# Twelve modulation blocks of the second layer moved out of the heads, border sums on VectorE, and a last residual by tokens

## The chip, the cores and the metric

One core of one Trainium2 chip runs one launch of the kernel. The metric is the time of the device in microseconds (us), the median over runs; less is better. Three runs of the kernel before gave a median of 1421.49 us (1420.72 to 1425.16).

## The reference

A block of two layers works on 256 tokens of x and 256 of a context, width 1024, all in float32. Cut to what matters:

```python
for l in range(DEPTH):                      # 0: HGRN mixer, 1: mamba mixer
    last = l == DEPTH - 1
    mx = split((silu(c) @ ada_w[l] + ada_b[l]), 6)          # modulation of x
    mc = split(silu(c_ctx) @ ada_w[l] + ada_b[l], 6)        # and of the context
    hx, hc = modulate(rmsnorm(x, pre[l,0]), mx[0], mx[1]), modulate(rmsnorm(ctx, pre[l,0]), mc[0], mc[1])
    yx, yc = mixer[l](hx, hc)
    x = x + mx[2] * rmsnorm(yx, post[l,0]);   ctx likewise with mc[2], if not last
    hx = modulate(rmsnorm(x, pre[l,1]), mx[3], mx[4])
    yx = (silu(conv(hx @ w_up[:, :2816])) * (hx @ w_up[:, 2816:])) @ w_down
    x = x + mx[5] * rmsnorm(yx, post[l,1]);   ctx likewise, if not last
return x                                     # 256 x 1024
```

ada_w is 2 x 1024 x 6144: 48 MB in all, or 24 blocks of 1024 x 512 (2 MB), twelve to a layer. Of each layer, columns 0 to 1023 are the shift before the mixer, then scale, gate, and the same three for the FFN.

## The kernel before, in words

**Layout.** Activations are held transposed: xT and yT are [128, 8, 512], 8 feature tiles of 128 by 512 tokens (256 of the context, 256 of x). From the mamba output on only the 256 tokens of x are left. Weights stream from HBM in pieces of 512 KB (two rows of tiles, `wraw`); ScalarE (ACT) rounds each to `wh` (`split_hi`, line 779), VectorE (DVE, line 1288) or GpSimd (POOL, line 654) takes the rest `wl`, and TensorE (PE) makes each product of float32 from three matmuls, hh·wh, hl·wh, hh·wl (lines 2052 to 2054, or 2067 to 2069 where the inputs arrive one by one).

**Order.** Everything is written out by hand. Each engine runs its own program, and a planner (`plan.add(key, bank, reader)`) only gives PSUM banks and the counts of the semaphores. Loads stand in one list on the queue of SP, each with a wait for its buffer; an engine's instructions run strictly in the order written.

**Stages.** (1) start, (2) eight heads of the HGRN mixer, some 42 us each, (3) its output product y0 to y7, then **border A**, the end of the mixer and the begin of FFN 0, (4) FFN 0, whose last tile opens **border B**, (5) mamba groups g = 0 to 7 with two steps more that drain the pipeline, (6) its output product (`("y", 1, m)`), **border C**, (7) FFN 1 with `up` and `down` in two halves, (8) the end: residual, transposition to rows of tokens, store.

**Modulation.** Block n goes through four steps. `load_ada(n)` on SP brings two halves of 1 MB into `araw`. `ada_block(n)` on PE multiplies the silu of the two conditions with it (line 2118, 8 instructions in the order of the program, 16 in the trace). `ada_rows(n)` copies the sums out (ACT, line 852). `ada_turn(n)` is four transposes on PE (line 2130), and `ada_add(n)` two small ones on DVE (lines 1298 and 1303) that finish `mod`. `norm_scales` and `gate_scales` then form nsc and gsc. How many blocks a head takes is in `ada_of`; those behind the heads are numbered from LATE on. `araw` and `scc` lie on the stack of the HGRN stage, so no block can stand behind it.

**Borders.** rmsnorm of the mixer's output, residual and the next rmsnorm are folded: three sums over features are needed, of y² (`ss`), of B = y·gsc·x (`sb`) and of A = (gsc·y)² (`sa`). For each tile m, ACT squares y (line 786) and gsc·y (`scaled_square`, line 823), DVE forms and adds up B (lines 1355 and 1360), POOL adds up the two squares (lines 709 and 718). PE sums over partitions with `ones` (lines 2340 and 2342). `variance` (lines 1369 to 1380) and `add_and_norm` (1393 to 1408) follow, and their first results release FFN's first matmul (line 2067).

**End.** `residual` forms y·rstd on 256 columns (line 1333, and 726 on POOL) and xT + gsc·that (line 1343) tile by tile; PE transposes 16 blocks (line 2588), ACT and DVE copy four banks, and SP stores two pieces of 512 KB.

Of the kernel before, what the change touches and what calls it, by code (L numbers as in the profile page):

```python
# [18 lines left out]
P = 128  # L19
# [113 lines left out]
def program(nc, a, out):  # L133
# [22 lines left out]
    gsc = sb(ctx, "gsc", [P, 2, 2, KT, 2])  # L156
    ident = sb(ctx, "ident", [P, P])
# [8 lines left out]
    mbs = sb(ctx, "mbs", [64, 3])  # L166
    asum = sb(ctx, "asum", [P, 2, 512])
# [16 lines left out]
    araw = sb(hg, "araw", [P, 2, 4, 512])  # L184
    scc = sb(hg, "scc", [P, KT, 32])
# [74 lines left out]
    ada_of = [1, 2, 2, 2, 2, 2, 2, 2]  # L260
# [86 lines left out]
    def plan_ffn(l):  # L347

        for half in range(2):
            ffp[l, half, "up"] = plan.loop(2 * FH[half], {"dve": 2 * FH[half]})  # L350
            if half == 0:
                if l == 0:
                    plan.add(("at", LATE + 3), 6, "dve")
                    plan.add(("at", LATE + 4), 7, "dve")
                ffp[l, half, "down"] = plan.loop(KT, {"act": KT})
            else:
                for m in range(KT):
                    plan.add(("fy", l, m), 4 + m % 2, "dve")

    plan_ffn(0)  # L360
    plan_sums(0, 1, (0, 1))
    ring = {"g": 0, "s": 0}
# [6 lines left out]
    for g in range(GROUPS + 2):  # L369
# [11 lines left out]
        if g == 1:  # L381
            mkey(("tk", 0), "dve")
# [7 lines left out]
        if G:  # L390
            gkey(("b", g), "dve")
        if S:
# [4 lines left out]
        if g == 0:  # L397
            plan.add(("c", g), 7, "dve")
        elif G:
            gkey(("c", g), "dve")  # L400
        if Q:
            mkey(("yt", q), "act")
        if S:
            mkey(("off", p, 0), "dve")
            mkey(("off", p, 1), "dve")
        if G:
# [3 lines left out]
    for m in range(KT):  # L410
        plan.add(("y", 1, m), m % 3, "act")
    plan_sums(1, 0, (4, 5))
    plan_ffn(1)
    plan.add(("ss", 1, 1), 7, "act")
    for half in range(2):
        for t in range(2):
            plan.add(("out", t, half), 2 * t + half, ("act", "dve")[half])
# [73 lines left out]
    scales, rsq_ready = sem("scales"), sem("rsq_ready")  # L491
    a_ready, a_added, b_added, var_ready = sem("a_ready"), sem("a_added"), sem("b_added"), sem("var_ready")
    x_new = sem("x_new")
    hf_ready, hh_ready, hl_ready = sem("hf_ready"), sem("hh_ready"), sem("hl_ready")
    yl_ready, odd_ready = sem("yl_ready"), sem("odd_ready")
# [21 lines left out]
    rows_act, rows_dve = sem("rows_act"), sem("rows_dve")  # L517
# [27 lines left out]
    def ada_half(n, half):  # L545
# [6 lines left out]
        return afirst[half], a_landed[half], 16 * (n - 1)  # L552
# [9 lines left out]
    def _(sp):  # L562
# [14 lines left out]
        def load_ada(n):  # L577

            l, c = ada_order[n] // 12, 512 * (ada_order[n] % 12)
            user = n - 2 if n <= ADA_FIRST else n - 1  # L580
            for half in range(2):
                if n == LATE + 4:
                    plan.wait_ready(sp, ("ot", HEADS - 1))
                elif user >= 0:
# [31 lines left out]
        load_ada(LATE + 4)  # L616
        for n in range(5 * HEADS + SLOTS + 4, len(subs)):
            load(n)
        for t in range(2):
            sp.wait_ge(rows_act, t + 1)  # L620
            sp.wait_ge(rows_dve, t + 1)
            sp.dma_start(out[0, t * P:(t + 1) * P, :], rows_out[:, t, :]).then_inc(stored, 16)
        sp.wait_ge(stored, 32)
# [3 lines left out]
    def _(pool):  # L627
# [29 lines left out]
        def split_rest(l, w):  # L657

            for half in range(2):
# [31 lines left out]
                else:  # L691
                    for m in range(KT):
                        add_square(2 * l + 1, m, w)
                        if l == 0:
                            add_scaled(1, m, w)
# [15 lines left out]
        def add_scaled(n, m, w):  # L711

            A = a_sums[n]
            if 1 <= m < KT - 1:
                pool.wait_ge(a_ready, KT * n + m + 1)
                if m > 1:
                    pool.wait_ge(a_added, (KT - 2) * n + m - 1)
                pool.tensor_tensor(A[m % 2][:, 0:w], A[m % 2][:, 0:w], A[1 - m % 2][:, 0:w], ALU.add).then_inc(a_added, 1)

        def scale_odd(n, w):  # L720

            pool.wait_ge(rstd_ready, 2 * n + 2)
            for m in range(1, KT, 2):
                if m >= 2:
                    pool.wait_ge(x_new, KT * n + m - 1)
# [1890 lines left out]
```

## Time and profile before

| | |
|---|---|
| runs (3) | median 1421.49 us, 1420.72 to 1425.16 |
| profiled execution | 1424.4 us, its span 1422.7 us |
| PE busy | 1332.8 us, 94% |
| DVE busy | 903.5 us, 64% |
| ACT busy | 660.9 us, 46% |
| POOL busy | 355.2 us, 25% |
| DMA | 183.15 MB, mean 129 GB/s |
| chain that ended last | PE 77%, DVE 11%, ACT 6%, DMA 3%, issue 2% |

All numbers of single instructions come from the profiled execution. Its time lies 2.9 us above the median, and 1.7 us of it lie outside the span. A row of the timeline reads: start in us from the span's start, duration in us, engine, line, operation, tiles out<-in, partitions x elements, count, and in brackets how long the engine sat idle before it and who released it. Matmuls overlap, so what one costs is the distance of starts, not its duration.

### The profile page before, as it was taken

To read this page: it belongs to the slowest core of one execution; us is meant where nothing else is said; L and a number is where in the kernel's file an instruction comes from. 1 tells how busy PE (TensorE), PEld (TensorE's weight loads), DVE (VectorE), ACT (ScalarE), POOL (GpSimd) and SP (SyncE) were. 2 spreads that over 40 slices of the span, in tenths; PEclk is the share of its full clock that TensorE was granted. 3 is DMA by queue.
4 is the path that set the end of the run, shared out by engine and by line. 5 is a ranking of instruction groups with operands and counts; after the bars stand their busy time and mean duration, and the time that the engine had idled before them with its cause. 6 is when DMAs were issued, how large, how long until landed. Compare 5 with 4: busy or idle time off the path is not lost.

```text
span 1422.7 us, 21240 instructions
## 1 busy us (share of the span) xinstructions
PE 1332.8 (94%) x7879; PEld 1119.1 (79%) x7879; DVE 903.5 (64%) x1678; ACT 660.9 (46%) x1050; POOL 355.2 (25%) x243
## 2 busy tenths in 40 slices
PE   5999999999987999999999978999999978899996
PEld 2677877777764788888888847888888877899996
DVE  5667765667759744422445788677777856764564
ACT  4444444444455633223333456555555645654552
POOL 1000000000231455104551500211111321681952
PEclk9999999999999999999999988999999989999998
DMA  9565445457542233234322324233333235456642
GB/s 346 168 193 178 160 137 178 130 182 236 179 161 76 74 106 94 74 96 118 97 83 63 104 59 114 80 89 90 101 92 90 74 90 149 119 162 186 198 137 86
DMA packets 274483, 183.15 MB, mean 129 GB/s; under 512 B 6595, under 2 KB 249059, under 8 KB 274403
## 3 DMA queue, kind: packets, MB, share of 16 engines
q1 hardware_dynamic: 273858, 180.00, 42.1%
q10 hardware_dynamic: 544, 2.10, 0.4%
q8 instruction: 49, 0.80, 0.2%
q14 instruction: 32, 0.25, 0.1%
HBM read 181.03 MB, written 1.05 MB: 128 GB/s over the span
## 4 chain that ended last, share of the span: by engine, by line
PE 77%; DVE 11%; ACT 6%; DMA 3%; issue 2%; SPq 1%; POOL 1%; POOLq 0%; DVEq 0%; ACTq 0%
PE bank L2052 20%; PE bank L2054 20%; PE bank L2053 20%; DVE wl L1288 2%; PE bank L2118 2%; ACT tmp L834 1%; DMA gates<-in_ada_w 1%; DMA araw<-in_ada_w 1%; ACT wh L779 1%; DVE hl L1388 1%; DVE tmp L1408 1%; PE bank L2167 1%; DVE conv L1739 1%; PE bank L2567 1%; PE bank L2542 1%
## 5 line engine op out<-in xcount | busy, mean ns | idle before, releaser
L2052 PE MATMUL bank<-hh,wh 128*128 128x512 f32 (+1 forms) x1305 | 464.9, 356 | 16.0 <-DVE wl L1288 10.8
L2054 PE MATMUL bank<-hh,wl 128*128 128x512 f32 (+1 forms) x1305 | 459.8, 352 | 0.0
L2053 PE MATMUL bank<-hl,wh 128*128 128x512 f32 (+1 forms) x1305 | 459.4, 352 | 0.0
L779 ACT ACTIVATE wh<-wraw 128x1024 fp32r<-128x1024 f32 (+2 forms) x265 | 256.3, 985 | 97.3 <-PE bank L2054 92.2
L2052 PEld LDWEIGHTS bank<-hh,wh 128*128 128x128 f32 x1305 | 249.6, 191 | 51.5 <-DVE wl L1288 13.6
L1288 DVE TENSOR_TENSOR wl<-wraw,wh 128x1024 fp32r<-128x1024 f32 (+2 forms) x187 | 209.8, 1144 | 124.6 <-ACT wh L779 124.6
L2054 PEld LDWEIGHTS bank<-hh,wl 128*128 128x128 f32 x1305 | 249.4, 191 | 33.1
L2053 PEld LDWEIGHTS bank<-hl,wh 128*128 128x128 f32 x1305 | 249.6, 191 | 30.8
L1739 DVE SCALAR_TENSOR_TENSOR conv<-bank,pv,conv 128x189 f32<-128x189 f32 (+3 forms) x396 | 173.2, 437 | 132.5 <-ACT conv L1056 104.3
L654 POOL TENSOR_TENSOR wl<-wraw,wh 128x1024 fp32r<-128x1024 f32 x78 | 187.1, 2408 | 236.4 <-ACT wh L779 235.8
L2052 PE MATMUL bank<-fh,wh 128*128 128x512 f32 (+1 forms) x352 | 119.7, 340 | 3.9 <-DVE wl L1288 3.5
L2054 PE MATMUL bank<-fh,wl 128*128 128x512 f32 (+1 forms) x352 | 119.0, 338 | 0.0
L2053 PE MATMUL bank<-fl,wh 128*128 128x512 f32 (+1 forms) x352 | 119.0, 338 | 0.0
L701 POOL TENSOR_TENSOR hl<-yT,hh 128x512 fp32r<-128x512 f32 x13 | 19.2, 1503 | 385.9 <-DVE gates L1635 374.8
L753 POOL TENSOR_TENSOR wx<-xtok,wtk 128x512 f32<-128x512 f32 x16 | 16.9, 1057 | 248.1 <-ACT xtok L1179 159.8
L2052 PEld LDWEIGHTS bank<-fh,wh 128*128 128x128 f32 x352 | 66.2, 188 | 12.5 <-issue 2.1
L2054 PEld LDWEIGHTS bank<-fh,wl 128*128 128x128 f32 x352 | 66.2, 188 | 8.0
L2053 PEld LDWEIGHTS bank<-fl,wh 128*128 128x128 f32 x352 | 66.2, 188 | 7.9
L2067 PE MATMUL bank<-hh,wh 128*128 128x512 f32 (+2 forms) x119 | 47.6, 400 | 21.1 <-DVE hl L1388 18.8
L674 POOL TENSOR_TENSOR fl<-prod,fh 128x512 f32 (+3 forms) x44 | 50.0, 1135 | 55.1 <-ACT fh L1072 55.1
L1056 ACT ACTIVATE conv<-bank,pv 128x512 f32<-128x512 f32 (+1 forms) x44 | 29.4, 668 | 71.7 <-PE bank L2054 71.7
L709 POOL TENSOR_TENSOR sq<-sq 128x512 f32<-128x512 f32 (+1 forms) x24 | 27.3, 1138 | 107.9 <-ACT sq L786 107.9
(325 smaller groups left out, 1960.5 us busy)
## 6 DMA issues: line engine op xcount, KB each, us to landing
wraw<-in_ffn_w_up SPq DMA_DIRECT2D x88, 512.0 KB, 3.9
araw<-in_ada_w SPq DMA_DIRECT2D x42, 1024.0 KB, 7.2
wraw<-in_mb_w_in SPq DMA_DIRECT2D x48, 512.0 KB, 4.0
wraw<-in_hg_w_in SPq DMA_DIRECT2D x40, 512.0 KB, 4.2
wraw<-in_ffn_w_down SPq DMA_DIRECT2D x32, 512.0 KB, 3.8
wraw<-in_mb_w_out SPq DMA_DIRECT2D x16, 512.0 KB, 4.2
gates<-in_ada_w SPq DMA_DIRECT2D x5, 1024.0 KB, 10.7
wraw<-in_hg_w_out SPq DMA_DIRECT2D x8, 512.0 KB, 5.9
```

The costliest lines, as they stand in the source:

```text
L654: pool.tensor_tensor(wl[:, n % SLOTS, 0:size], wraw[:, n % SLOTS, 0:size], wh[:, n % SLOTS, 0:size].bitcast(F32), ALU.subtract).then_inc(w ...
L674: pool.tensor_tensor(fl[:, bass.ds(i * 2 + c, 1), 0:w], prod[:, c % 2, 0:w].unsqueeze(1), fh[:, bass.ds(i * 2 + c, 1), 0:w].bitcast(F32), ...
L709: pool.tensor_tensor(sq[:, m % 2, 0:w], sq[:, m % 2, 0:w], sq[:, 1 - m % 2, 0:w], ALU.add).then_inc(sq_added, 1)
L779: act.activation(wh[:, n % SLOTS, 0:size], wraw[:, n % SLOTS, 0:size], ACT.Copy).then_inc(w_hi, 1)
L1056: act.activation(conv[:, u, 0:n], bank[2 * u if src is None else src][:, 0:n], ACT.Identity, scale=pv[:, bass.ds(i * 2 + (cw + c), 1)], bi ...
L1288: ins = dve.tensor_tensor(wl[:, s, lo:hi], wraw[:, s, lo:hi], wh[:, s, lo:hi].bitcast(F32), ALU.subtract)
L1739: ins = V.scalar_tensor_tensor(out=o(conv[:, u, :]), in0=src(bank[up]), scalar=pv[:, bass.ds(i * 2 + (cw + row * FT + c), 1)], in1=o(conv[ ...
L2052: pe.matmul(dst, W, hi(k), start=(k == 0), stop=False, **skip)
L2053: pe.matmul(dst, W, lo(k), start=False, stop=False, **skip)
L2054: ins = pe.matmul(dst, L, hi(k), start=False, stop=(k == nk - 1), **skip)
L2067: pe.matmul(dst, W, hi(k), start=(k == 0), stop=False, skip_group_check=True)
L2118: ins = pe.matmul(bank[plan.bank(key)][32 * j:32 * j + 32, :], scc[:, 4 * half + j, :], raw[:, j, :], start=(half == 0), stop=(half == 1))
```

## The change

1. `ada_of` is [1, 1, 1, 1, 1, 1, 1, 1], so LATE falls from 19 to 12. The blocks LATE to LATE+4 stay at the places of the program where five stood before. Seven more get places: LATE+5 and +6 behind the sums of border B (turns in g = 0, before and behind project("c")), LATE+7 in g = 1, LATE+8 in g = 8, LATE+9 in g = 9 (turn behind y tile 1), LATE+10 behind y tile 1 (turn behind tile 3), LATE+11 ahead of FFN 1 (turn after its first `up` half). Their loads are put into SP's list behind given weight loads (`after`). `araw` and `scc` lie below all stages now. LATE+6 lands in `rows_out`, `prod` and `tmp`.
2. At the three borders DVE forms A itself, from ACT's y² and gsq = gsc², and adds up y²: lines 1370 and 1381 of the changed kernel. `scaled_square`, `add_scaled` and POOL's `add_square` there go, and so does one of PE's two sum matmuls for A. At border A the splits of y tiles 5 to 7 stand one tile earlier, as far as they did not already.
3. At the end ACT scales y by gsc into `conv`, PE transposes that (two 128x128 a tile, `y_rows`) and xT (`x_rows`, four for each of tiles 0 to 3) inside the `down` loop, ACT copies the latter to rows_out. The sum of squares comes out per token (four matmuls of one column, `token_sums`), ACT's Ln and Exp work on 128x2, four DVE instructions of 128x512 form bank·rstd + rows_out, and four stores of 256 KB follow.

The diff, cut to its core:

```diff
-    ada_of = [1, 2, 2, 2, 2, 2, 2, 2]
+    ada_of = [1, 1, 1, 1, 1, 1, 1, 1]
...
+        after = {at["up", 0, 0, 0, 0] + 12: (LATE + 5,), at["down", 0, 1, 0, 0] + 7: (LATE + 6,), at["z", 0, 0]: (LATE + 7,),
+                 at["z", 2, 0]: (LATE + 8,), at["m", 3, 1]: (LATE + 9, LATE + 10), at["m", 4, 1]: (LATE + 11,)}
         for n in range(5 * HEADS + SLOTS + 4, len(subs)):
             load(n)
+            for late in after.get(n, ()):
+                load_ada(late)
...
-                        if l == 0:
-                            scaled_square(1, 0, 1, m, n)
+                        if l == 1:
+                            if m >= 2:
+                                act.wait_ge(gy_used, m - 1)
+                            act.activation(conv[:, m % 2, 0:n], yT[:, m, 0:n], ACT.Copy, scale=gsc[:, 1, 1, m, 0:1])\
+                                .then_inc(gy_ready, 1)
+                            if m < 4:
+                                t, h = m // 2, m % 2
+                                key = ("xr", t, h)
+                                plan.wait_ready(act, key)
+                                plan.empty(act.activation(rows_out[:, t, h * 512:h * 512 + 512], bank[6][:, :], ACT.Copy), "act", key)
...
-                step(ins)
-                step.wait()
-                ins = V.tensor_tensor(B[m % 2][:, 0:n], B[m % 2][:, 0:n], B[1 - m % 2][:, 0:n], ALU.add)
-            ins.then_inc(b_added, 1)
+                product = step(ins)
+            else:
+                ins.then_inc(b_added, 1)
+            A, S = a_sums[i], sq[:, m % 2, :]
+            dve.wait_ge(sq_ready, KT * i + m + 1)
+            if m:
+                dve.wait_ge(a_added, KT * i + m)
+            for b in range(n // SEQ):
+                r = slice(b * SEQ, (b + 1) * SEQ)
+                g2 = gsq[:, l, s, m, b:b + 1]
+                if m:
+                    ins = V.scalar_tensor_tensor(out=A[m % 2][:, r], in0=S[:, r], scalar=g2, in1=A[1 - m % 2][:, r],
+                                                 op0=ALU.mult, op1=ALU.add)
+                else:
+                    ins = V.tensor_scalar(A[0][:, r], S[:, r], g2, None, ALU.mult)
+            ins.then_inc(a_added, 1)
+            if 1 <= m < KT - 1:
+                step.wait(product)
+                V.tensor_tensor(B[m % 2][:, 0:n], B[m % 2][:, 0:n], B[1 - m % 2][:, 0:n], ALU.add).then_inc(b_added, 1)
+                dve.wait_ge(a_added, KT * i + m + 1)
+                if m > 1:
+                    dve.wait_ge(sq_added, (KT - 2) * i + m - 1)
+                V.tensor_tensor(S[:, 0:n], S[:, 0:n], sq[:, 1 - m % 2, 0:n], ALU.add).then_inc(sq_added, 1)
...
+                if (l, s, m) == (0, 1, 0):
+                    plan.wait_ready(dve, ("am", LATE + 6))
...
-        residual(1, 1, SEQ)
+        dve.wait_ge(rstd_ready, rn[0] + 1)
+        plan.wait_emptied(dve, ("xr", 1, 1))
+        for half in range(2):
+            for t in range(2):
+                key = ("out", t, half)
+                plan.wait_ready(dve, key)
+                o = rows_out[:, t, half * 512:half * 512 + 512]
+                plan.empty(V.scalar_tensor_tensor(out=o, in0=bank[plan.bank(key)][:, :], scalar=rstd[:, t:t + 1], in1=o,
+                                                  op0=ALU.mult, op1=ALU.add), "dve", key)
...
@@ down loop of ffn_pe @@
+                            ada_block(LATE + 5)
+                            ada_block(LATE + 6)
...
+                        if l == 1:
+                            if m < 4:
+                                x_rows(m // 2, m % 2)
+                            if 1 <= m < KT - 1:
+                                y_rows(m - 1)
                     if l == 1:
-                        y_square_sum(("ss", l, 1), n)
+                        token_sums()
+                        y_rows(KT - 2, [("out", t, 0) for t in range(2)])
+                        y_rows(KT - 1, [("out", t, 1) for t in range(2)])
```

How the rows of the engines' programs move, at three places.

PE in the second of the heads, around the turn and the block that stand between the projections and `o_turn` (line 2225; `asum` is the block's sum copied out, `tmp` the head's output). Before:

```order
L2054 MATMUL bank<-hh,wl 128x512
L2130 MATMUL bank<-ident,asum 128x128 x4
L2118 MATMUL bank<-araw,scc 32x512 x8
L2225 MATMUL bank<-ident,tmp 128x128 x4
L2167 MATMUL bank<-gates 128x128 x4
```

and now, with the lines of the changed kernel:

```order
L2094 MATMUL bank<-hh,wl 128x512
L2170 MATMUL bank<-ident,asum 128x128 x4
L2265 MATMUL bank<-ident,tmp 128x128 x4
L2207 MATMUL bank<-gates 128x128 x4
L2212 MATMUL bank<-qx,kx 32x32 x8
```

The second block of the head is gone there; further down its turn goes as well. So in each of seven heads.

DVE at border A, two tiles of the output product (`gates` holds the sums A and B there). Before:

```order
L1355 SCALAR_TENSOR_TENSOR gates<-yT,gsc,xT 128x256 x2
L1360 TENSOR_TENSOR gates<-gates 128x512
L1288 TENSOR_TENSOR wl<-wraw,wh 128x1024
L1355 SCALAR_TENSOR_TENSOR gates<-yT,gsc,xT 128x256 x2
L1360 TENSOR_TENSOR gates<-gates 128x512
L1288 TENSOR_TENSOR wl<-wraw,wh 128x1024
```

and now:

```order
L1355 SCALAR_TENSOR_TENSOR gates<-yT,gsc,xT 128x256 x2
L1370 SCALAR_TENSOR_TENSOR gates<-sq,gsq,gates 128x256 x2
L1377 TENSOR_TENSOR gates<-gates 128x512
L1381 TENSOR_TENSOR sq<-sq 128x512
L1312 TENSOR_TENSOR wl<-wraw,wh 128x1024
```

Per tile DVE has three instructions more, two of 256 columns and one of 512.

DVE at the end, from the last partial sums of `down` on. Before:

```order
L1785 TENSOR_TENSOR yT<-bank,yT 128x256 x3
L1333 TENSOR_TENSOR tmp<-yT,rstd 128x256
L1343 SCALAR_TENSOR_TENSOR xT<-tmp,gsc,xT 128x256
L1333 TENSOR_TENSOR tmp<-yT,rstd 128x256
L1343 SCALAR_TENSOR_TENSOR xT<-tmp,gsc,xT 128x256 x2
```

and now:

```order
L1810 TENSOR_TENSOR yT<-bank,yT 128x256 x3
L2079 SCALAR_TENSOR_TENSOR rows_out<-bank,rstd,rows_out 128x512 x4
```

Twelve instructions of 256 columns and two copies of 512 give way to four of 512.

## Rows read from the trace of the kernel before

**Rows 1.** The page: busy time of each engine, share of the span, instructions.
```profile
PE 1332.8 (94%) x7879; PEld 1119.1 (79%) x7879; DVE 903.5 (64%) x1678; ACT 660.9 (46%) x1050; POOL 355.2 (25%) x243
```

**Rows 2.** Windows of five heads, 209 us: busy time of each engine, summed, and the mean.
```profile
sum 209.00, PE 208.46 PEld 165.24 DVE 140.59 ACT 94.54 POOL 0.00; mean PE 41.69 PEld 33.05 DVE 28.12 ACT 18.91 POOL 0.00
```

**Rows 3.** Timeline of PE in the heads, around blocks and turns.
```profile
211.58 1.92 PE L2118 MATMUL bank<-araw,scc 128*32 128x512 f32 x16
213.43 0.82 PE L2194 MATMUL bank<-vtok,ket 128*128 128x128 f32 x5
...
222.11 1.06 PE L2118 MATMUL bank<-araw,scc 128*32 128x512 f32 x8 [0.83 <-DMA araw<-in_ada_w]
223.11 0.65 PE L2225 MATMUL bank<-ident,tmp 128*128 128x128 f32 x4
...
232.21 0.60 PE L2130 MATMUL bank<-ident,asum 128*128 128x128 f32 x4
232.64 0.61 PE L2204 MATMUL bank<-vtok,gates 128*128 128x128 f32 x4
```

**Rows 4.** Timeline of DVE in the same head: what `o_turn` (L2225) reads and who reads it.
```profile
218.19 0.68 DVE L1551 TENSOR_TENSOR tmp<-bank,osm 128x512 f32<-128x512 f32 x1
...
223.80 0.75 DVE L1559 SCALAR_TENSOR_TENSOR yT<-bank,pv,gs 128x512 f32<-128x512 f32 x1 [3.08 <-PE bank L2225]
```

**Rows 5.** Timeline of DVE at border A.
```profile
410.59 0.88 DVE L1355 SCALAR_TENSOR_TENSOR gates<-yT,gsc,xT 128x256 f32<-128x256 f32 x2
...
423.90 2.94 DVE L1355 SCALAR_TENSOR_TENSOR gates<-yT,gsc,xT 128x256 f32<-128x256 f32 x2
426.88 1.67 DVE L1360 TENSOR_TENSOR gates<-gates 128x512 f32<-128x512 f32 x1
...
436.58 0.69 DVE L1360 TENSOR_TENSOR gates<-gates 128x512 f32<-128x512 f32 x1
437.19 1.22 DVE L1288 TENSOR_TENSOR wl<-wraw,wh 128x1024 fp32r<-128x1024 f32 x1
```

**Rows 6.** Timeline of POOL at border A.
```profile
425.09 1.48 POOL L718 TENSOR_TENSOR gates<-gates 128x512 f32<-128x512 f32 x1
```

**Rows 7.** Timeline of PE at border A.
```profile
424.04 0.50 PE L2052 MATMUL bank<-hh,wh 128*128 128x512 f32 x1 [2.30 <-DVE wl L1288]
...
443.73 1.02 PE L2342 MATMUL bank<-gates,ones 128*128 128x512 f32 x2
...
451.70 0.47 PE L2067 MATMUL bank<-hh,wh 128*128 128x512 f32 x1 [3.38 <-DVE hl L1388]
```

**Rows 8.** Timeline of PE: idle time at border B, in mamba and at border C.
```profile
834.31 0.77 PE L2067 MATMUL bank<-hh,wh 128*128 128x512 f32 x1 [8.09 <-DVE hl L1388]
883.87 0.68 PE L2443 MATMUL bank<-ident,dtf 64*128 64x64 f32 x4 [2.50 <-DVE dg L1858]
1125.59 0.89 PE L2515 MATMUL bank<-wx,btok 128*128 128x256 f32 x2 [1.39 <-POOL wx L755]
1157.16 0.58 PE L2052 MATMUL bank<-hh,wh 128*128 128x256 f32 x1 [3.38 <-DVE wl L1288]
1202.55 0.55 PE L2067 MATMUL bank<-hh,wh 128*128 128x256 f32 x1 [5.96 <-DVE hl L1388]
```

**Rows 9.** Windows: busy PE, PEld, DVE, ACT, POOL; granted clock of PE, DMA share, GB/s.
```profile
884.00:890.30 6.30, 6.30 (x23) 5.16 (x24) 4.78 (x11) 0.00 (x0) 0.00 (x0) 0.50 0.98 275
1150.00:1160.00 10.00, 5.77 (x25) 5.48 (x26) 5.25 (x5) 6.07 (x10) 2.91 (x3) 0.50 0.23 67
1380.60:1406.30 25.70, 25.70 (x214) 25.69 (x215) 12.00 (x20) 11.12 (x19) 4.42 (x6) 1.00 0.44 129
```

**Rows 10.** Timeline of the end: DVE and SP's queue.
```profile
1409.13 0.99 DVE L1333 TENSOR_TENSOR tmp<-yT,rstd 128x256 f32<-128x256 f32 x1 [2.25 <-ACT rstd L802]
...
1418.30 1.19 SPq L622 DMA_DIRECT2D out_x<-rows_out  x2
```

**Rows 11.** The page, DMA issues: tiles, count, KB each, median us to landing.
```profile
araw<-in_ada_w SPq DMA_DIRECT2D x42, 1024.0 KB, 7.2
```

More of the change, by code:

```diff
@@ L358, in plan_ffn @@
                     plan.add(("fy", l, m), 4 + m % 2, "dve")
+                    if l == 1 and m < 4:
+                        plan.add(("xr", m // 2, m % 2), 6, "act")
     plan_ffn(0)
     plan_sums(0, 1, (0, 1))
+    plan.add(("am", LATE + 5), 6, "act")
+    plan.add(("am", LATE + 6), 5, "act")
     ring = {"g": 0, "s": 0}
@@ L416, in program @@
         for t in range(2):
-            plan.add(("out", t, half), 2 * t + half, ("act", "dve")[half])
+            plan.add(("out", t, half), 2 * t + half, "dve")
     subs, done_at, lo_of, at = [], [], [], {}
@@ L1267, in _ @@
         shift_high(1, 1, SEQ)
+        ada_rows(LATE + 11)
         ffn_act(1, SEQ, False)
-        rsqrt(("ss", 1, 1), SEQ, D)
-        for t in range(2):
-            key = ("out", t, 0)
-            plan.wait_ready(act, key)
-            act.activation(rows_out[:, t, 0:512], bank[plan.bank(key)][:, :], ACT.Copy).then_inc(rows_act, 1)
+        key = ("ss", 1, 1)
+        plan.wait_ready(act, key)
+        plan.empty(act.activation(rstd[:, 0:2], bank[7][:, 0:2], ACT.Ln, scale=1.0 / D, bias=eps[:, 0:1]), "act", key)
+        plan.wait_emptied(act, key)
+        act.activation(rstd[:, 0:2], rstd[:, 0:2], ACT.Exp, scale=-0.5).then_inc(rstd_ready, 1)
     @block.vector
@@ L1775, in ffn_dve @@
                         ada_add(LATE + 4)
+                    else:
+                        ada_add(LATE + 11)
+                        step.wait()
+                        gate_scales(1, 1)
                 else:
@@ L1999, in _ @@
                     weights(p, i)
+            if g == 0:
+                ada_add(LATE + 5)
             if G:
@@ L2032, in _ @@
             products(2, 1, 0, m, SEQ)
+            if m == 2:
+                ada_add(LATE + 9)
+                step.wait()
+                norm_scales(1, 1)
+            if m == 4:
+                ada_add(LATE + 10)
         variance(1, 0, SEQ)
@@ L2390, in ffn_pe @@
                 plan.passed(fills=2 * nf)
-                if l == 0 and half == 0:
-                    ada_turn(LATE + 3)
-                    ada_turn(LATE + 4)
+                if half == 0:
+                    for n0 in ((LATE + 3, LATE + 4), (LATE + 11,))[l]:
+                        ada_turn(n0)
                 r0, reads = ffp[l, 0, "down"]
```

222 lines of the change are left out of this document (120 added, 102 removed).

## The prediction

> **What bounds the kernel now.** I read the page first: PE is busy 1332.8 of 1422.7 us, 94%, the next engine 64% [rows 1]. So work taken off PE counts in full wherever PE has no idle time, and work laid on it is free only in its gaps. Second the windows of the heads: in 209 us of five heads PE is busy 208.5, DVE 141 and ACT 95 [rows 2]. Third PE's timeline there, for the price of a block and of a turn [rows 3]. Fourth the borders, where PE's bracket names what it waited for [rows 5 to 8]; fifth the granted clock around these gaps [rows 9]; last the end [rows 10].
>
> **Heads.** Seven of the eight heads lose one block and one turn. A block costs PE the distance from its start to the next instruction, 213.43 - 211.58 = 1.85 us, a turn 232.64 - 232.21 = 0.43 [rows 3]; 7 x 2.28 = **16.0 us**. The second block of that head waited 0.83 for its load [rows 3], and it is the block that goes; I count such waits as 1.4 in all heads, from nothing to 3. What is late next? PE would come to the transposes of L2225 some 3.1 us (1.85 + 0.43 + 0.83) before 223.11, at 220.0; their input is ready at 218.19 + 0.68 = 218.87 [rows 3, 4]. There are 1.1 us to spare. DVE has a third of a head free [rows 2], and its two small instructions and ACT's copy per block leave too. I take **-17.4**, between -12 (a chain of DVE and ACT eats a quarter) and -19.
>
> **Border A.** While POOL adds (1.48 us each) DVE's pair L1355 takes 2.94 and its addition L1360 1.67; free of POOL, ahead of its first and behind its last, they take 0.88 and 0.69 [rows 5, 6]. So DVE, with a split of 1.22 at its best, needs over 6 us a tile, PE's 24 matmuls less, and PE stands 2.30 us for `wl` [rows 7]. After the change POOL has nothing to add. DVE does 0.88 + 0.88 (the A pair, priced as its equal) + 0.69 + 0.69 = 3.1 a tile, 4.3 with a split, and PE is no longer held. But the sums then close on DVE alone: from 410.6 on [rows 5] eight tiles (7 x 3.1 + 1.7) and six splits (7.3) make 30.5, so 441.1, half a microsecond less where no split waits; PE's last sum follows at once and ends near 442, where the last now ends at 443.73 + 1.02 = 444.75 [rows 7]. I take **-3.0**. The ends are 0 (DVE's new load just fills what contention took) and -6 (all of PE's waits and of the tail of the sums).
>
> That rests on the contention. The Trainium skill states it in "SBUF — State Buffer", section "Who interferes with whom": a VectorE instruction with two inputs in SBUF and a GpSimd instruction that reads SBUF exclude each other, and the later one blocks. By "Perfetto Trace Analysis", "Optimizing Scalar/DVE Operations", giving GpSimd work of a saturated VectorE may make sense, though the shared port may spoil it; by its first half this change goes the wrong way and border A would lose DVE's extra 1.6 us a tile, 13 us. The rows at hand side with the first page.
>
> **Other borders.** At B the last tile's sum costs one matmul less, -0.3. In the output product of mamba ACT has one instruction less per tile ahead of the splits; of the 3.38 idle [rows 8] I take -0.5. At C both may fall to nothing; 0.
>
> **Blocks in their new places.** LATE+5 and +6 (3.7 us) stand in 8.09 idle at border B, LATE+11 in 5.96 at border C, LATE+10 in the 3.38 of the y tiles, where the last blocks have their turns as well [rows 8], LATE+9 in the drain ahead of it: free, while these gaps last. LATE+7 stands ahead of dt_turns, in the 2.50 idle that DVE sets, free too. LATE+8 (1.85) meets 1.39 idle: +0.5. Turns within full streams cost 0.43 to 0.55 each, for LATE+7, +8 and +10: +1.6. DVE's two small instructions in its gapless stretch before 883.87 (LATE+5 and +6), priced at their counterparts' size: +0.7, a choice between 0 and 1. ACT's copy for LATE+11 ahead of FFN 1's activations: +0.5, taken the same way. Together **+3.3**, from +1 to +6.
>
> **The clock.** PE's granted clock is 0.50 from 884.0 to 890.3, right after it idled 2.50 us, and from 1150 to 1160 [rows 8, 9]; 0.50 is 1.2 GHz, 1.00 is 2.4. Border A's 3.38 idle, behind two blocks, was followed by full speed. Blocks now stand in the gaps ahead of 884 and 1157. Half of PE's busy time in a slow stretch is lost: 6.30 / 2 = 3.2 us at 884, 5.77 / 2 = 2.9 in the y tiles. I take **-4.0** of 6.1; the ends are 0 and -6.
>
> The Trainium skill's "TensorE: Matmul & The Clock Gate", Part 1, has it that the throttled state is the default and activity lifts it; so filling a gap should keep the clock. By the opposite reading, that a block of a few matmuls of 32 columns is too little, the sum would be without its 4.0.
>
> **The end.** PE's `down` loop is full, 25.70 of 25.70 [rows 9]. It gets 16 + 12 transposes; at 0.43 for four that is 3.0, and 3.9 with a little for each of the ten switches between kinds of work. ACT gets a scaling on each tile and a copy on four (by DVE's rows for such sizes, an estimate, 0.4 and 0.7), ahead of the splits of the coming tiles; I add 1.5 for PE waits, 0 to 4. So +5.4. Behind the last tile: DVE's residual begins at 1409.13, the first store is issued at 1418.30, the second some 0.8 later [rows 10], 10 us. Now four instructions like L1559, 0.75 each [rows 4], are 3.0, and the last store goes out right behind. That is -7, and -0.85 for Ln and Exp on two columns and a store of half the size. Net **-2.4**, between -6 and +2.
>
> **Sum.** -17.4 - 3.0 - 0.8 + 3.3 - 4.0 - 2.4 = -24.3. On the profiled execution's 1424.4 us that gives 1400.1; on the median, 2.9 lower, 1421.5 - 24.3 = **1397.2**.
>
> **Rivals.**
>
> *Clock not held, or the down loop bound by ACT.* The blocks in the gaps don't keep the clock (+4.0) and PE waits for splits in four tiles of `down` (+3): 1404. For it: 32 columns are little work, and PE had just stood. Against: border A.
>
> *The heads don't give the time back.* DVE and ACT are only 67% and 45% busy, but their chains are in order, and 1.1 us of slack at L2225 is not much. If each head returns half, 8.7 is missing: 1406. Against: PE shows no idle time of that kind in these heads.
>
> *Better.* Border A gives 6, the clock 6, the loop costs 1.5 less: 1391.
>
> *Slower: the loads hold the weights back.* Each late block adds 2 MB to SP's list, in which weights for the next tiles queue behind, and the second half waits until the block before has been used. A half takes 7.2 us to land [rows 11]. The places are dense: LATE+9 and +10 stand behind the same weight load. Were PE to wait 7.2 for each of the seven, that is +50 on top: 1447; from 3.5 us a block on the change loses (24.3 / 7). For it: at 884 the DMA engines are already 0.98 busy, where LATE+7 loads. Against: in the y stage they are 0.23 busy [rows 9], and the loads stand several stages ahead of their blocks.
>
> *The change doesn't do what it says*: border A's DVE work fills the gap exactly and the end stays as it is: 1397 + 3 + 2.4 = 1402, within the range.
>
> **Chances.** Forecast 0.60, clock or loop 0.17, heads 0.10, better 0.08, slower 0.05. A measurement of this kernel can tell 0.3%, 4.3 us. All cases but the last lie more than that below 1421.5; of the last, and of mixtures of two others, I give 0.03 to within 0.3%. So faster 0.93, same 0.03, slower 0.04. The range 1387 to 1410 takes in the bounds of the terms as they would add up by chance and the middle rivals, and leaves out the last and the corners.
>
> **What would show it.** Right: windows of a head about 2.3 to 2.5 us shorter with PE full; L1355 at 0.87 in every tile of border A and no wait for `wl` there; the first matmul of FFN 0 some 3 us sooner behind the same work; granted clock 1.00 behind 884; about 3 us from rstd to the last store. Wrong: a new idle time in the heads ahead of L2225's or the gates' matmuls; idle time of PE before a block with a DMA as its releaser, or before weights with ACT `wh` where DMA had been late; PE below full in the `down` loop. The forecast as a whole is wrong if the heads give less than 12 or blocks wait for their loads by more than a microsecond each.

## The result, and the profile after

The changed kernel takes **1403.82 us** (median of 4 runs, 1403.17 to 1405.46), the kernel before beside it 1423.33 (1420.72 to 1425.80): ratio 0.9862, 95% interval 0.9844 to 0.9880. It is 19.5 us faster; a later comparison gave 1404.80 against 1425.13, ratio 0.9854 (0.9839 to 0.9869). The forecast was 24.3 less, 1397.2, in a range from 1387 to 1410. The direction and the range held. The gain is 4.8 us short of the forecast; the other 1.8 of the distance to 1397.2 is that the kernel before has a median of 1423.33 here, and 1421.49 in the runs that the forecast started from. One thing that no part of the forecast contained cost more than what is missing: 6.9 us, as the first experiment shows.

The page of the kernel after, which answers to [rows 1]:

```profile
span 1401.9 us, 21260 instructions
...
PE 1330.2 (95%) x7893; PEld 1118.4 (80%) x7893; DVE 901.2 (64%) x1730; ACT 646.8 (46%) x1020; POOL 305.0 (22%) x203
```

PE's busy time fell by only 2.6 us though the span fell by 20.8: no work left PE, it was put where PE had been idle. POOL lost 50 us of work, and DVE, which took over its sums, is no busier than before. That fits a DVE that had been held up; border A below shows it.

**Where the time went, stage by stage.** I laid the two traces side by side at instructions that both have, and took the difference of their starts:

| place | start before | start after | ahead by | this stage |
|---|---|---|---|---|
| last transposes of the heads (L2225, now L2265) | 403.61 | 386.99 | 16.6 | +16.6 |
| first matmul of FFN 0 | 451.70 | 430.15 | 21.6 | +4.9 |
| first matmul behind border B | 834.31 | 812.53 | 21.8 | +0.2 |
| turns of dt in g = 1 | 883.87 | 862.81 | 21.1 | -0.7 |
| scoring of g = 1 (second pair of L2467, now L2542) | 902.20 | 884.62 | 17.6 | -3.5 |
| third tile of mamba's output | 1157.16 | 1140.97 | 16.2 | -1.4 |
| first matmul of FFN 1 | 1202.55 | 1185.53 | 17.0 | +0.8 |
| last matmul of `down` | 1406.07 | 1394.10 | 12.0 | -5.0 |
| end of the span | 1422.7 | 1401.9 | 20.8 | +8.8 |

**Heads.** The windows of five of them, which answer to [rows 2], span 196 us and not 209, and PE is full in each (two rows and the sum; columns as in [rows 9]):

```profile
94.20:133.40 39.20, 39.20 (x251) 32.17 (x250) 24.79 (x54) 18.35 (x31) 0.00 (x0) 1.00 0.36 116
133.40:172.60 39.20, 39.20 (x253) 32.22 (x253) 27.91 (x60) 18.36 (x32) 0.00 (x0) 1.00 0.38 121
...
sum 196.00, PE 196.00 PEld 161.06 DVE 136.46 ACT 91.75 POOL 0.00; mean PE 39.20 PEld 32.21 DVE 27.29 ACT 18.35 POOL 0.00
```

A head now takes 39.2 us, 2.4 to 2.5 less, and the slack at the turn that follows held (the five windows leave out one head between the third and the fourth, which is full too). On DVE's timeline of after, which answers to [rows 4], `tmp` starts at 212.64, some 0.8 us before L2265 at 214.12 needs it complete:

```profile
212.64 0.68 DVE L1573 TENSOR_TENSOR tmp<-bank,osm 128x512 f32<-128x512 f32 x1
```

**Border A.** DVE's timeline of after for one tile (answers to [rows 5]):

```profile
411.13 0.88 DVE L1355 SCALAR_TENSOR_TENSOR gates<-yT,gsc,xT 128x256 f32<-128x256 f32 x2
411.93 0.87 DVE L1370 SCALAR_TENSOR_TENSOR gates<-sq,gsq,gates 128x256 f32<-128x256 f32 x2
412.72 0.68 DVE L1377 TENSOR_TENSOR gates<-gates 128x512 f32<-128x512 f32 x1
413.32 0.68 DVE L1381 TENSOR_TENSOR sq<-sq 128x512 f32<-128x512 f32 x1
413.92 1.22 DVE L1312 TENSOR_TENSOR wl<-wraw,wh 128x1024 fp32r<-128x1024 f32 x1
```

With twice the pairs and one addition more, a tile takes 3.9 us with its split, where before one pair and one addition next to POOL took 4.6 without it. On PE (answers to [rows 7]) the waits for `wl`, of 2.30 and of 1.05 behind it, are gone, and a new one stands at the sums:

```profile
418.07 1.10 PE L2402 MATMUL bank<-sq,ones 128*128 128x512 f32 x2 [2.57 <-DVE sq L1381]
...
430.15 0.76 PE L2107 MATMUL bank<-hh,wh 128*128 128x512 f32 x1 [3.98 <-DVE hl L1408]
```

**What was not foreseen** stands on PE's timeline in g = 1 and g = 8:

```profile
862.81 0.46 PE L2518 MATMUL bank<-ident,dtf 64*128 64x64 f32 x4 [1.37 <-DVE dg L1880]
...
866.04 0.46 PE L2527 MATMUL bank<-dg,ones 64*128 64x96 f32 x2 [2.40 <-DVE cbm L1973]
...
884.62 0.50 PE L2542 MATMUL bank<-ahl,identr 128*128 128x256 f32 x2 [1.41 <-DVE ared L1322]
...
1118.88 0.63 PE L2170 MATMUL bank<-ident,asum 128*128 128x128 f32 x4 [1.09 <-DVE wd L1921]
```

The first row is the wait of 2.50 of [rows 8], now 1.37 with a block ahead of it. The other three waits did not exist before, and none of them is for data: the matmul L2527 reads `dg` and `ones`, and `dg` was ready at 862.76, yet it starts only behind DVE's second `cbm` instruction, which reads the bank of PSUM that another operation had filled. DVE's timeline:

```profile
862.53 0.23 DVE L1880 TENSOR_SCALAR dg<-ident,mbs 64x32 f32<-64x32 f32 x1
...
865.58 0.41 DVE L1973 TENSOR_TENSOR cbm<-bank,ident 128x256 f32<-128x256 f32 x1
```

Ahead of L2527 the program of PE has one wait, `plan.wait_free(pe, ("cd",))`, the wait for its bank. The turn in the last row reads `asum`, and waits for DVE's `wd`. They are waits for a **bank**.

The wait of the first row is of another kind. Its transposes read `dtf`, `elf` and `atf`, which DVE had finished ahead of three splits of `wl` (858.95 to 862.45), but the program waits with `pe.wait_ge(dt_dve, 4)`, and the fourth count comes with `dg`, behind those splits. So part of the idle time of 2.50 that the forecast took as set by DVE's work is set by where the program counts; no run moved it.

**The end.** DVE's and SP's timelines of after (answer to [rows 10]):

```profile
1396.65 2.73 DVE L2079 SCALAR_TENSOR_TENSOR rows_out<-bank,rstd,rows_out 128x512 f32<-128x512 f32 x4 [1.73 <-ACT rstd L1297]
```

```profile
1397.43 2.31 SPq L668 DMA_DIRECT2D out_x<-rows_out  x4
```

### The profile page after: what moved, and what is told of

It is laid out like the page before. It is cut to its first block, busy times and chain, and to the rows that moved or that the text cites. A ratio compares the mean times of both kernels' runs of the same rounds, so it can differ in the third digit from the quotient of the medians.

```text
span 1401.9 us, 21260 instructions
## 1 busy us (share of the span) xinstructions
PE 1330.2 (95%) x7893; PEld 1118.4 (80%) x7893; DVE 901.2 (64%) x1730; ACT 646.8 (46%) x1020; POOL 305.0 (22%) x203
## 3 DMA queue, kind: packets, MB, share of 16 engines
HBM read 181.03 MB, written 1.05 MB: 130 GB/s over the span
## 4 chain that ended last, share of the span: by engine, by line
PE 77%; DVE 13%; ACT 6%; issue 2%; DMA 1%; SPq 1%; POOL 0%; DVEq 0%; ACTq 0%
PE bank L2092 20%; PE bank L2094 20%; PE bank L2093 20%; DVE wl L1312 3%; ACT tmp L845 1%; DMA gates<-in_ada_w 1%; PE bank L2158 1%; ACT wh L799 1%; DVE hl L1408 1%; DVE tmp L1430 1%; PE bank L2207 1%; DVE conv L1760 1%; PE bank L2234 1%; PE bank L2654 1%; ACT hh L849 1%
## 5 line engine op out<-in xcount | busy, mean ns | idle before, releaser
L1312 DVE TENSOR_TENSOR wl<-wraw,wh 128x1024 fp32r<-128x1024 f32 (+2 forms) x187 | 206.0, 1123 | 122.4 <-ACT wh L799 122.3
L2093 PEld LDWEIGHTS bank<-hl,wh 128*128 128x128 f32 x1305 | 249.1, 191 | 30.7
L777 POOL TENSOR_TENSOR wx<-xtok,wtk 128x512 f32<-128x512 f32 x16 | 16.9, 1055 | 252.4 <-ACT xtok L1197 162.1
L2107 PEld LDWEIGHTS bank<-hh,wh 128*128 128x128 f32 (+1 forms) x119 | 24.1, 203 | 30.4 <-issue 11.0
```

The source lines that it names most:

```text
L777: pool.tensor_tensor(hd(wx[d][:, 0:2, :], 2), hd(xtok[:, 2:4, :], 2), scale(wtk, 2, 2), ALU.mult)\
L1312: ins = dve.tensor_tensor(wl[:, s, lo:hi], wraw[:, s, lo:hi], wh[:, s, lo:hi].bitcast(F32), ALU.subtract)
L2093: pe.matmul(dst, W, lo(k), start=False, stop=False, **skip)
L2107: pe.matmul(dst, W, hi(k), start=(k == 0), stop=False, skip_group_check=True)
```

## The experiments

All are variants of the changed kernel. Kernels of one group ran on one chip and share the runs of the kernel before.

### Banks of their own for two blocks (x_ring)

In mamba, PSUM banks 3 to 6 are dealt out in turn (`mkey`), and LATE+7 and LATE+8 each took two places in that turn. All later operations of the ring were thereby shifted.

```diff
-            mkey(("am", LATE + 7), "act")
+            plan.add(("am", LATE + 7), 7, "act")
...
-            mkey(("at", LATE + 7), "dve")
+            plan.add(("at", LATE + 7), 7, "dve")
...
-            mkey(("am", LATE + 8), "act")
+            plan.add(("am", LATE + 8), 2, "act")
...
-            mkey(("at", LATE + 8), "dve")
+            plan.add(("at", LATE + 8), 2, "dve")
```

> The changed kernel, with banks of their own for the blocks LATE+7 (bank 7, for its sums and its turn) and LATE+8 (bank 2) in place of two places each in the ring of banks 3 to 6, so that all other operations get back the banks they had before the change. Theory 1 (the ring): the two steps shifted by one put the matmul of `cd` on the bank that VectorE's two `cbm` instructions still read (PE idle 2.40), the second row matmul on the bank of the turn just made (1.41), and the turn of LATE+8 on the bank of a row that VectorE reads late (1.09). All three go: 4 to 5 us less than the changed kernel, about 1399. Theory 2 (VectorE or the work itself): VectorE is late there in any case and the waits only move: within 1 us of the changed kernel's 1403.8.

Measured: **1396.97 us** (1395.65 to 1398.80), before 1424.41, ratio 0.9814 (0.9795 to 0.9834). That is 6.9 below the changed kernel. PE's timeline at the same places:

```profile
864.95 0.46 PE L2518 MATMUL bank<-ident,dtf 64*128 64x64 f32 x4 [1.38 <-DVE dg L1880]
...
865.62 0.41 PE L2527 MATMUL bank<-dg,ones 64*128 64x96 f32 x2
...
880.35 0.82 PE L2542 MATMUL bank<-ahl,identr 128*128 128x256 f32 x4
...
1113.68 0.60 PE L2170 MATMUL bank<-ident,asum 128*128 128x128 f32 x4
```

All three waits are gone and nothing has taken their place, with the same instructions in the same order. Theory 1 holds, theory 2 falls. From L2518 to the turn L2170 this trace gains 7.3 on that of the changed kernel: 4.9 are the three waits, 0.3 a fourth short one, 1.6 the clock, which fell to 0.50 behind the 2.40 us wait there and did not here, and 0.5 is left over. The windows (after; this kernel):

```profile
866.00:870.30 4.30, 4.26 (x12) 3.38 (x13) 1.76 (x6) 0.00 (x0) 0.00 (x0) 0.60 0.70 193
```

```profile
865.00:870.00 5.00, 5.00 (x30) 4.21 (x31) 4.79 (x11) 0.00 (x0) 0.00 (x0) 1.00 1.08 298
```

This is no luck of one pair. In all four traces of kernels with the two blocks in the ring (the changed kernel, its repetition, x_old_sums and x_old_end) the wait of 2.40 stands there, and the clock fell in it or right behind it, at a cost of 1.7, 2.7, 3.3 and 1.7 us. In all five with banks of their own and this block (x_ring, y_u2_late, y_xr_early, y_both, z_two_late) neither is there. So the banks cost 4.9 us directly and 1.7 to 3.3 through the clock, which is why the gain is more than the 4 to 5 expected.

### The blocks back into the heads (x_heads2)

```diff
-    ada_of = [1, 1, 1, 1, 1, 1, 1, 1]
+    ada_of = [1, 2, 2, 2, 2, 2, 2, 2]
```

and no block, turn, copy, addition, load or bank at LATE+5 to LATE+11.

> The changed kernel with two blocks in seven heads again and none at the seven late places; border sums and end as changed. Theory 1: the heads give 17.5 us and the late places cost about 5 of it, so this one is 12 to 13 us slower than the changed kernel, about 1416.5; in the profile the heads are 17.5 us longer and all of mamba 5 us shorter. Theory 2 (late places free, the missing time is elsewhere): 17 us slower, 1421.

Measured: 1417.49 us (1416.66 to 1419.48), ratio 0.9957 (0.9940 to 0.9974); 13.7 slower than the changed kernel. In the traces the changed kernel is 19.8 us ahead in the last head (at 360.6 of this one), 14.0 behind the scoring of g = 1 and 15.8 at the end; this profiled execution is 2 us above its median. So seven blocks give 19.8 (7 x 2.45 = 17.2, two waits for loads, and the clock, which differs between the two) and cost 4 to 6 in their new places, the 4.9 of the banks among it. Theory 1. The forecast had 3.3 for those places, and the clock on the other side.

### The borders' sums as before (x_old_sums)

ScalarE's `scaled_square`, GpSimd's two additions and the two matmuls for A put back at all three borders, with the old order of the splits.

> The changed kernel with the sums of all three borders made as before (ScalarE squares gsc*y, GpSimd adds up both squares, two matmuls for A). Theory 1 (GpSimd and VectorE exclude each other): VectorE's pair L1355 is back at 1.9 to 2.9 us beside GpSimd, PE waits for wl at border A, the first FFN matmul comes 4 us later, another 1 us is lost at borders B and C: 4 to 5 us slower, about 1408.5. Theory 2 (VectorE's new load costs as much as it frees): within 1.5 us of 1403.8.

Measured: 1408.73 us (1406.36 to 1411.06), ratio 0.9897 (0.9879 to 0.9916); 4.9 slower. DVE's and PE's timelines at border A:

```profile
406.04 2.92 DVE L1390 SCALAR_TENSOR_TENSOR gates<-yT,gsc,xT 128x256 f32<-128x256 f32 x2
409.00 1.67 DVE L1395 TENSOR_TENSOR gates<-gates 128x512 f32<-128x512 f32 x1
```

```profile
406.17 0.79 PE L2109 MATMUL bank<-hh,wh 128*128 128x512 f32 x1 [2.71 <-DVE wl L1347]
```

The same pair of instructions that takes 0.88 us without GpSimd's additions takes 2.92 with them, and the wait for `wl` is back. From the last transposes of the heads to FFN 0's first matmul it is 48.09 us as before the change, and 43.16 with it. So the gain at the borders, 4.9, lies at border A. How much of it the earlier splits of tiles 6 and 7 have was not run apart from the sums.

### The end as before (x_old_end)

The residual over 128x256 tiles, the transposes behind it and two stores of 512 KB put back, and nothing added to the down loop.

> The changed kernel with the end of before (residual over 128x256 tiles, transposes after it, two stores of 512 KB, nothing added to the down loop). Theory 1: the loop of the last down products gets 4.3 us shorter and what follows it 8.6 us longer, so 4 to 4.5 us slower, about 1408. Theory 2 (my forecast's 2.4): 1406.2.

Measured: 1407.71 us (1405.71 to 1409.68), ratio 0.9890 (0.9872 to 0.9908); 3.9 slower. DVE's and SP's timelines:

```profile
1392.69 0.99 DVE L1356 TENSOR_TENSOR tmp<-yT,rstd 128x256 f32<-128x256 f32 x1 [2.25 <-ACT rstd L829]
...
1401.07 0.69 DVE L2099 COPY rows_out<-bank 128x512 f32<-128x512 f32 x1 [1.21 <-PE bank L2670]
```

```profile
1401.86 1.19 SPq L666 DMA_DIRECT2D out_x<-rows_out  x2
```

From the last `down` matmul to the end it is 16.6 us here and 7.8 in the changed kernel, which ends its own loop 4.5 later: 4.2 net in the traces. Theory 1, within half a microsecond.

The three parts undone one by one are worth 13.7, 4.9 and 3.9, together 22.5; the change as a whole 19.5 to 20.3, by its two comparisons with the kernel before. Each of these numbers compares runs of different groups and is good to some 2 us; within that they add up.

### One block more in the heads, none in g = 1 (y_heads13)

On top of x_ring:

```diff
-    ada_of = [1, 1, 1, 1, 1, 1, 1, 1]
+    ada_of = [1, 2, 1, 1, 1, 1, 1, 1]
```

and the place of LATE+7 empty; the blocks behind it move down one number.

> The ring kernel with one block more in the heads (two in the second head, so thirteen blocks before the end of HGRN) and none in g = 1; LATE+8's block of before on bank 2 as there. Theory 1 (a block in a head costs PE its full 2.3 to 2.45 us, the place in g = 1 about 1.2: half of the block in VectorE's 2.50 us gap, and the turn): 1 to 1.5 us slower than the ring kernel's 1397.0, about 1398.3, with head 1 longer by 2.4 and the stretch around dt_turns shorter by 1.2. Theory 2 (the place in g = 1 is as dear as a head, since VectorE ends the gap anyway): equal within 0.5.

Measured: 1400.04 us (1399.26 to 1402.45), before 1424.68, ratio 0.9836 (0.9820 to 0.9852); 3.1 slower than x_ring, twice the expected; the intervals of the two ratios overlap a little, so the traces must decide. The head costs its 2.4 there (2.5 from 93.6 to 108.1 us). What failed is the other side: the block in g = 1 costs nothing, and only its turn does, 0.4 further on. Its trace shows PE idle 3.22 where x_ring has the block and 1.38, and then the clock at half:

```profile
866.08 0.46 PE L2511 MATMUL bank<-ident,dtf 64*128 64x64 f32 x4 [3.22 <-DVE dg L1875]
```

```profile
866.00:871.00 5.00, 4.92 (x22) 4.04 (x23) 4.79 (x12) 0.00 (x0) 0.00 (x0) 0.66 1.03 292
```

So a block there is paid for out of idle time, 1.9 of block and 1.4 of idle for 3.2 of idle. And the clock, which stayed at 1.00 in the five traces with the block and its own banks, fell here behind the longer gap; that side is one execution, and the last runs show how little one execution says.

### A split behind the last products, transposes of xT ahead of the loop (y_u2_late, y_xr_early, y_both)

On top of x_ring. The first moves the split of FFN 0's third piece:

```diff
-... (at["y", 0, 7],), (), (u0,), (u0 + 1,), (u0 + 2,), ())):
+... (at["y", 0, 7],), (), (u0,), (u0 + 1,), (), (u0 + 2,))):
```

the second takes three of four `x_rows` out of the down loop, to banks 6 and 7:

```diff
+                if l == 1:
+                    for t, h in (((0, 0),), ((0, 1), (1, 0)))[half]:
+                        x_rows(t, h)
...
-                            if m < 4:
-                                x_rows(m // 2, m % 2)
+                            if m == 0:
+                                x_rows(1, 1)
```

> The ring kernel with VectorE's split of the third piece of FFN 0 behind its products of the last tile at border A instead of ahead of them. Theory 1 (border A is now bound by VectorE's chain, PE idle 2.57 us ahead of the sums): the last products start 1.1 us sooner and the split falls in VectorE's idle 1.21 us before line 1389: FFN 0 starts 1.0 us sooner, about 1396. Theory 2 (ScalarE's squares or the sums' matmuls bound it): 0 to 0.3.

> The ring kernel with three of the four sets of transposes of xT out of the last down loop: one at the seam between up and down of the first half (copied by VectorE later), two at that of the second half, where PE idles 1.55 us (copied by ScalarE ahead of its last gate). Theory 1 (each costs PE 0.5 us in the full loop plus 0.3 of waits, and nothing in the seams): 2.0 to 2.5 us faster, about 1394.7. Theory 2 (ScalarE's chain sets the pace of the loop and of the seam, whichever work it has): 0 to 0.7, or slower where the copies delay the gate and with it fl.

> The ring kernel with both of these. If they are independent, as they lie 900 us apart, their gains add up: about 1393.7.

Measured: 1396.59 (1395.08 to 1396.80), 1395.54 (1394.62 to 1395.88) and 1396.19 us (1395.48 to 1397.33), ratios 0.9806 (0.9791 to 0.9820), 0.9797 (0.9783 to 0.9812) and 0.9807 (0.9793 to 0.9822). None differs clearly from x_ring's 1396.97; their intervals overlap. The expected 1396.0, 1394.7 and 1393.7 are missed by 0.6, 0.8 and 2.5, and the gains did not add up. The traces say more than the medians. The moved split gave **nothing** at border A: from the last transposes of the heads to FFN 0 it is 43.17 us, and 43.16 in the changed kernel (44.60 in x_ring's own trace, in which the clock fell in the sums at 418 us). My reading of what bounded it was wrong: DVE's last products did start sooner, but PE's first sum still waited for the same instruction,

```profile
416.62 1.10 PE L2402 MATMUL bank<-sq,ones 128*128 128x512 f32 x2 [2.57 <-DVE sq L1381]
```

the addition of squares of the last tile but one, ahead of which this split never stood. The early transposes shortened the stretch from FFN 1's first matmul to the end by 1.4 (216.43 to 215.05): PE's idle time before `down` fell from 1.52 and 1.55 to 1.09 and 0.67, so the seams absorbed three sets, and the wait of 0.49 in the loop went. Two more short waits for ACT's `conv`, of 0.26 to 0.28, came in its place. That is below the 2.0 to 2.5 expected, and the median moved by 1.4.

### Two splits behind the last products; both kernels again (z_two_late, z_after_again, z_before_again)

z_two_late is y_both with the second piece's split moved behind the last products as well. The other two are the changed kernel and the one before as they are.

> The ring kernel with the early transposes of xT, and now two splits (second and third piece of FFN 0) behind VectorE's products of the last tile. The run with the third alone showed why it gave nothing at border A: what ends the wait of PE's first sum is the addition of squares of the last tile but one (line 1381), and that stands ahead of the third split in either order. Theory 1 (VectorE's chain through this addition): the second split stands ahead of it, so PE's first sum comes 1.1 us sooner after the last o_turn (30.0 us in place of 31.1) and FFN 0 too; about 1.0 us below the kernel with early transposes, 1394.5. Theory 2 (the last tile's square or PE bounds it): no difference.

> The changed kernel once more, beside the others on one chip: 1403.8, within 1 us, if the comparison across calls holds. Its trace tells whether the half-clock stretches at 88, 358 and 430 us come with the kernel (there again, each of them) or with the execution (some of them gone); in the other traces so far the stretch at 88 us came and went between kernels whose program up to there is the same.

> The kernel before once more: 1423 to 1425. Half-clock stretches at 829, 866, 883, 1126, 1149 and 1201 us again if they come with the program, and one at 89 us if that one is a matter of the execution, since PE idles 2.34 us there in this kernel as well.

Measured: z_two_late **1394.58 us** (1393.43 to 1395.90), before 1425.13, ratio 0.9788 (0.9775 to 0.9801). Its first sum comes 30.01 us after the last transposes of the heads, where it was 31.1, as expected:

```profile
417.24 1.10 PE L2415 MATMUL bank<-sq,ones 128*128 128x512 f32 x2 [1.52 <-DVE sq L1391]
```

FFN 0 starts 42.09 us after them, for 43.17. Theory 1; the time alone would not tell it from y_xr_early and y_both. It is the fastest kernel of the study, 10.2 us below the changed one and 30.6 below the one before, all three on one chip; some seven of the 10.2 are the banks.

z_after_again 1404.80 (1402.82 to 1405.90), z_before_again 1424.09 (1422.03 to 1426.79, ratio 0.9996, 0.9985 to 1.0007). Their traces show what a half-clock stretch is worth as evidence. In the changed kernel's repetition all three stretches (88, 358 and 430 us) are there again. In that of the kernel before the one at 883 is gone and two new ones stand at 89 and 377. The windows of before and of before again at the seam of g = 0 and 1, which is the first of [rows 9], and in the first head:

```profile
88.00:92.00 4.00, 3.18 (x17) 2.77 (x18) 2.64 (x5) 2.23 (x4) 0.00 (x0) 1.00 1.05 402
```

```profile
90.00:94.00 4.00, 4.00 (x12) 3.16 (x11) 2.72 (x5) 1.26 (x3) 0.00 (x0) 0.58 1.08 368
883.00:890.00 7.00, 4.48 (x29) 3.66 (x28) 6.93 (x13) 2.27 (x4) 0.00 (x0) 1.00 0.87 228
```

The same program has the clock down at 884 and up at 88 in one execution, and the other way round in the other. Other stretches come with the program: the one at 358 us, in the last head, stands in all ten traces of kernels with one block there, and in one of the three with two blocks (this repetition, at 377), behind the same idle time of 2.4 us.

## Why the prediction was right, and where it was wrong

**Heads: right.** Forecast 17.4; at 360.88 us of the trace before the lead was 17.6. At 403.61 it was 16.6. The difference is the half-clock stretch at 358 us that the trace after has and the one before has not, 1.5 us of which part is made up behind it. All ten traces with one block in the last head have it (above), so it is more likely a cost of the change than of the execution, and one that the forecast did not have. The block's 1.85, the turn's 0.43 and 0.1 to 0.2 between kinds of work make the 2.45 that the traces show for a head. The 1.1 us of slack at L2225 shrank and held, since DVE's and ACT's share of each block left as well. The rival of the heads falls.

**Border A: mechanism right, size low.** Forecast 3.0, measured 4.9 (43.16 for 48.09, and x_old_sums returns exactly there). The term "eight tiles and six splits make 30.5" was mis-sized: from its first product to its last DVE took 26.8 us (393.82 to 420.64). The six splits and eight tiles are there as forecast, but what follows a pair of 0.87 starts 0.80 behind it, what follows an addition of 0.68 starts 0.60 behind it, and 1.13 for a split of 1.22: instructions overlap. A tile with a split is 3.9 and not 4.3. I had priced DVE by durations and PE by distances of starts; both want distances. That is some 2.5 us; another 1.6 is that the first tile has no additions, which its price of 3.1 had (it took 1.32); 0.3 goes back for a block's two small instructions in between. The sum itself was off by a little too: 7 x 3.1 + 1.7 + 7.3 is 30.7, and 2.94 + 1.67 + 1.22 is 5.8 and not over 6. The trace has 6.8 for that tile, since its split takes 2.31 as well. The contention as such is shown by x_old_sums, 2.92 against 0.88 for one pair, and within the trace before, where the pair behind GpSimd's last addition is back at 0.87. The reading by which the change goes the wrong way, 13 us lost at border A, falls.

**Blocks in their places: the step that failed.** "LATE+7 stands ahead of dt_turns, in the 2.50 idle that DVE sets, free too" and "LATE+8 meets 1.39 idle: +0.5". The block's work was indeed free: y_heads13 shows that the one in g = 1 costs nothing by itself. But each block also took two places in the ring of four PSUM banks, and moved what came behind it onto banks whose readers were late. I had followed what each block adds to the engines and to SP's queue, and not to the allocator; the diff showed it in four lines of `mkey`. It cost 4.9 us of waits and, through the clock, 1.7 to 3.3 more. x_ring takes it out and lands at 1396.97, where the forecast had 1397.2. That near agreement is luck: as a gain it is 27.4 us on the kernel before of its chip, where the forecast had 24.3. Border A's 1.9 and the end's 1.5 too little stand against a clock term that the traces do not bear out.

The forecast named "a new idle time of PE before a block with a DMA as its releaser" as the thing to fear. In the trace after no block behind the start of the kernel waits for its load, no matmul of the late stages waits for a DMA, and the rival of the held-up weights falls.

**The clock: not confirmed.** Forecast 4.0 at two places. Summing PE's busy time times the missing share of the clock over windows of 1 us, from 60 us on, gives 18.2 us lost in the trace before and 16.9 in its repetition; 14.7 and 17.1 in those of the changed kernel. 2.0 of before's are the end, which no longer runs at half. What is left is smaller than the difference between two executions of one program. Nor is all that is lost time of the kernel: the 1.7 of before at 866 us lie ahead of a wait for `wl` that is 0.17 there and 1.67 in the trace after, which ran at full clock.

The forecast's two places apart: its sign of being right, a clock of 1.00 behind 884, failed in the changed kernel, where the wait for a bank stands. With banks of their own the clock held in five traces of five. But with the gap empty, 2.50 to 2.52 us of idle, it fell in one trace of three only (3.2 us in the one before; not in its repetition nor in x_heads2). In the y tiles 2.9 and 4.4 us were lost in the two executions before, 2.5 and 2.7 in those of the changed kernel, so the blocks did not keep the clock up there. The 4.0 was read from a single execution; what a filled gap gives back on average is not settled by so few.

**The end: mechanism right, 1.5 too small, both halves off by 1 or less.** The loop cost 4.5 by x_old_end (forecast 5.4; the 5.0 of the table run from FFN 1's first matmul on), what follows gave 8.8 (forecast 7.85). Net 3.9 by the medians, forecast 2.4. The loop's tiles with both kinds of transposes lie 4.67 us apart for 3.61 before; PE waits 0.49, 0.26 and 0.29 for ACT in three of them, 1.0 where the forecast had 1.5.

**Borders B and C, y tiles.** Forecast 0.8, measured 0.2 at B and about 1 around C with the blocks that were hidden there: too small to be told.

The rivals: "clock not held or loop bound by ACT", 1404, is next to the measured number, and for another reason: PE waits for ACT for 1.0 us of the loop and no more, and the clock fell behind waits for banks; had I taken it for confirmed from the time alone, the banks would have stayed hidden.

## What to carry to other kernels

An operation that is put into a gap takes a buffer as well as time. Where buffers are dealt out in turn, it moves all that come behind it in the turn: give it one of its own, or follow who reads each bank last. On the trace, a wait whose releaser writes none of the waiting instruction's operands is a wait for a buffer, or for a count that comes later than the data; the program's wait ahead of the instruction tells which (L2527 and L2518 above).

Work taken from a second engine and given to a busier one can make the busier one faster, if the two exclude each other. And a clock state seen in one execution is no property of the program until others show it: the stretch at 884 was in one of three, the one at 358 in ten of ten.

## What the runs showed of the hardware that was not expected

PE's granted clock fell to 0.50 in one execution and not in the next, at the same instruction, behind the same idle time: behind 2.34 to 2.38 us in the first head it stayed at 1.00 in the trace before, in x_old_sums and in y_u2_late, and fell in the other ten, the repetition of before and both of the changed kernel among them. Each fall costs 1.4 to 1.7 us where it is short. From 60 us to the end of an execution the lost time lay between 11.7 (y_u2_late, whose profiled span of 1393.3 is 1.5 under the median of its spans) and 20.3 us (x_heads2). That is as large as most of the single gains of this study, so gains of one or two microseconds were read from distances between two instructions and not from a whole time.

VectorE pays for GpSimd's additions by the instruction: at border A a pair of 0.88 takes 1.92 to 2.94, an addition of 0.69 takes 1.67 and a split of 1.22 takes up to 2.31, about 1.0 us more for most of the single instructions, beside GpSimd's of 1.46 to 1.5 each. A tile of VectorE's pair and addition grew by 3.0 (from 1.57 to 4.6), as much as GpSimd's two additions a tile take, and its split by 1.1 on top. The Trainium skill's page "SBUF — State Buffer", section "Who interferes with whom", has the port pair that the two share as an exclusive lock, and the order of issue as what decides who blocks. The rows agree in that VectorE's pair, addition and split, which all have two inputs in SBUF, are all longer beside GpSimd; which engine held the lock they do not show.
